# How many cache pages each unit of the prompt's attention takes: by its blocks, or by what its blocks leave of an even share

## The reference

```python
# prompt: 4 heads x 8 blocks of 128 queries, causal
s = einsum('bqhmd,bkhmd->bmhqk', q, k) * scale + bias(q_pos - k_pos)
p = softmax(s); attn = p[:, 0] - lam * p[:, 1]; out = attn @ v
# the 8 sequences ("decode"): the same, on 4096 cached tokens each
kp = cache_k[l][page_table]   # 32 pages of 128 tokens a sequence
vp = cache_v[l][page_table]
```

## Time and profile before

| what | us |
|---|---|
| median of three runs (lowest, highest) | 1438.85 (1438.1, 1441.78) |
| the profiled execution | 1434.25 |
| its span | 1432.4 |
| TensorE busy in the span | 1269.2 |
| VectorE busy | 626.4 |
| ScalarE busy | 369.1 |
| waits of VectorE for key pages, 620 to 880 us | 31.0 |

### The profile page before, as it was taken

How to read it: one execution, slowest core, us unless ns; L and a number is a source line. 1 busy time by engine, 2 the same in 40 slices (tenths; PEclk the granted TensorE clock), 3 DMA queues, 4 the chain that set the end, 5 groups by cost and what they waited for, 6 DMA issues and landing times.

```text
span 1432.4 us, 24206 instructions
## 1 busy us (share of the span) xinstructions
PE 1269.2 (89%) x9261; PEld 897.7 (63%) x9261; DVE 626.4 (44%) x1464; ACT 369.1 (26%) x758; POOL 123.5 (9%) x300
## 2 busy tenths in 40 slices
PE   6999998999898989986687877999897399999987
PEld 5666876667687778744454545455554288787852
DVE  4001415444464638366576775455424511212117
ACT  4021202111212225244355553222222011111113
POOL 4400000000000010110000000000000111111012
PEclk9999999999999999988798988999998599999998
DMA  7810011010020106776877979999980499999837
GB/s 244 291 52 30 30 38 36 30 61 1 17 74 18 45 7 216 233 256 200 289 246 266 314 270 351 385 317 338 320 272 31 148 313 304 300 307 302 281 118 303
DMA packets 158308, 274.03 MB, mean 191 GB/s; under 512 B 13448, under 2 KB 72752, under 8 KB 158208
## 3 DMA queue, kind: packets, MB, share of 16 engines
q1 hardware_dynamic: 139776, 217.46, 45.1%
q0 software_dynamic: 11648, 38.39, 7.7%
q10 hardware_dynamic: 6784, 16.85, 3.4%
HBM read 235.55 MB, written 37.09 MB: 190 GB/s over the span
## 4 chain that ended last, share of the span: by engine, by line
PE 70%; DVE 12%; SPq 5%; DMA 4%; ACT 4%; issue 4%; POOL 0%; DVEq 0%; ACTq 0%; POOLq 0%
PE bank L1060 16%; PE bank L1063 13%; PE bank L1484 10%; PE bank L1343 6%; PE bank L1504 4%; PE bank L1109 4%; DVE arena L1762 3%; DMA arena<-in_cache_k_dram 3%; PE bank L1186 3%; SPq L527 3%; PE bank L1229 2%; ACT arena L875 2%; PE bank L1037 1%; PE bank L1499 1%; PE bank L1469 1%
## 5 line engine op out<-in xcount | busy, mean ns | idle before, releaser
L1060 PE MATMUL bank<-arena 128*128 128x352 f32 x768 | 239.0, 470 | 0.0
L1762 DVE STREAM_TRANSPOSE arena<-arena 128x512 f32<-128x512 f32 x256 | 158.4, 677 | 95.3 <-DMA arena<-in_cache_k_dram 95.0
L1060 PEld LDWEIGHTS bank<-arena 128*128 128x128 f32 x768 | 147.4, 195 | 80.1 <-issue 5.9
L1063 PE MATMUL bank<-arena 128*128 128x256 f32 (+1 forms) x864 | 195.5, 384 | 0.6 <-issue 0.6
L1063 PEld LDWEIGHTS bank<-arena 128*128 128x128 f32 (+1 forms) x864 | 155.0, 182 | 33.2 <-issue 6.3
L1484 PEld LDWEIGHTS bank<-arena 128*128 128x128 f32 x1024 | 143.2, 193 | 9.2 <-issue 9.2
L1484 PE MATMUL bank<-arena 128*128 128x160 f32 x1024 | 144.2, 303 | 1.9 <-DVE arena L2074 1.9
L1343 PE MATMUL bank<-arena 128*128 128x512 f32 x256 | 121.0, 617 | 0.9 <-ACT arena L885 0.9
L1186 PE MATMUL bank<-arena,tab 128*32 128x256 f32 x1024 | 71.1, 424 | 17.0 <-DVE arena L1762 11.6
L741 ACT ACTIVATE arena<-bank 128x352 f32<-128x352 f32 x48 | 22.2, 463 | 232.1 <-PE bank L1060 232.1
L1343 PEld LDWEIGHTS bank<-arena 128*128 128x128 f32 x256 | 47.4, 195 | 54.8 <-issue 54.5
(11 more groups left out here) (342 smaller groups left out, 1494.3 us busy)
## 6 DMA issues: line engine op xcount, KB each, us to landing
arena<-in_cache_k_dram SPq DMA_DIRECT2D x256, 256.0 KB, 4.7
arena<-in_cache_v_dram SPq DMA_DIRECT2D x256, 256.0 KB, 4.0
arena<-in_expert_w_dram SPq DMA_DIRECT2D x48, 1024.0 KB, 7.5
arena<-in_w_in_dram SPq DMA_DIRECT2D x14, 1024.0 KB, 5.0
expert_scratch<-route POOLq DMA_DIRECT2D x40, 256.0 KB, 6.9
expert_scratch<-arena ACTq DMA_DIRECT2D x16, 512.0 KB
out_dram<-arena SPq DMA_DIRECT2D x12, 512.0 KB, 3.0
arena<-in_x_prompt_dram SPq DMA_DIRECT2D x4, 1024.0 KB, 9.2
```

Source lines behind the costliest of these rows:

```text
L1060: mm = nc.tensor.matmul(bank(g)[:, 0:N3], w[:, k, c * P:(c + 1) * P], hT[:, k * TOK + n * N3:k * TOK + (n + 1) * N3], start=(k == 0), stop ...
L1063: mm = nc.tensor.matmul(bank(g)[0:ROWS[c], 0:256], tok(hT, k, c), w[:, k, :], start=(k == 0), stop=(k == KC - 1))
L1762: V.transpose(page, page).then_inc(sem("k_flip"), 1)
```

## The change

`u_beat` is computed from another share. A unit's share of pages falls in a straight line with i, by 0.44 a block from (4.5 x 0.44 + 62/32), with a floor of 0.25; units of two parts halve it; the sum is scaled to the same 62 beats. All else, the order of the quads in the ring and the two other lists too, is as before.

```diff
-        blocks = [sum(units[n][1] + 1 if units[n][1] < 4 else 4 if part == 0 else units[n][1] - 3 for n, part in parts[:k + 1]) for k in range(len(parts))]
-        u_beat = [v_beat[-1] + round(62 * n / blocks[-1]) for n in blocks]
+        def share(i):
+            return (4.5 - i) * 0.44 + 62 / len(units)
+
+        pages_of = [max(share(units[n][1]), 0.25) / (2 if units[n][1] >= 4 else 1) for n, part in parts]
+        u_beat = [v_beat[-1] + round(62 * sum(pages_of[:k + 1]) / sum(pages_of)) for k in range(len(parts))]
```

## The result

The change makes the kernel slower: 1448.44 us (median of 7 executions, 1439.14 to 1453.99) against 1438.1 for the kernel before (7 executions of the same session). The ratio is 1.0078, with a 95% interval of 1.0044 to 1.0111, or some 11 us. The forecast was 1416 in a range of 1395 to 1440, so it was wrong in sign. One of all the executions in this document was slow and is left out of its kernel's figures (e18: 1562.42 us, at a mean clock of 0.815 where the others had 0.935 to 0.948).

What follows compares the result with a forecast made beforehand. No engine fills a head: late key pages and a three-engine chain take turns. Heads -23 us, residual waits +4, mixing entry -4 make -23: 1434.25 becomes 1411, plus 4.6 for the median 1416, range 1395 to 1440.

Steps and rivals of the forecast that it cites:

- residual waits: Attention heads: waits for keys that would remain after the change, 1 us a head, plus 4 us in the sum.
- the chain: Units 2 to 5: combine, biases, transposed quad, exps take turns on three engines; each first-part quad adds 2.49 us.
- Fewer beats in units 5 to 7.: Head 2: unit 5 minus 3 us; units 6 and 7, with four beats fewer, minus 4.3.
- Entry of the mixing.: Start of the mixing stage: a ring left full by unit 7 gives back 0 to 7.9 us, 4 taken.
- The wait of 4.99 goes, since the ring was refilled during large units with few beats.: Unit 2 of head 2: VectorE's 4.99 us wait for keys disappears; the unit's net is minus 0.5 us.
- no change: Rival, chance 0.10: transfers pause in units 5 to 7, waits return in units 1 to 3, 6 us a head; 1436.
- The batch's end comes here. That costs 0 to 3.7, I take 2.: Unit 2 of head 2: the batch's softmax flips and previous batch's keep move here from unit 5, plus 2 us.
- Head 1.: Minus 12 us: wait -9, unit 0 +1.3, unit 1 +3, chain -5, units 6 and 7 -4.3, batch's end +2.
- Head 0.: Minus 5 us: units 0 and 1 get six quads and take about 20, plus 11; later units give more back.
- Head 3 has the same counts: Head 3 was taken to have head 2's counts of beats and quads, so also minus 3 us.
- VectorE piles up: Rival, chance 0.12: quads ahead of combine in units 0 to 2 make TensorE wait; +24 us, 1463.
- The clock: Rival, chance 0.10: waits in units 0 and 1 lower TensorE's clock in heads 1 to 3, +5 us each; 1431.

Runs made afterwards that it cites:

- e18: e10 with every key quad transposed two beats ahead of its own beat (three for the first of a pair): 1418.85 us, ratio 0.9897.
- e5: The kernel before with a quarter of every page loaded (32 of 128 rows): 1405.59 us, ratio 0.9779.
- e7: The kernel before with a quarter of each key page transposed (128 of 512 columns): 1404.59 us, ratio 0.9764.
- e13: The kernel before with a quarter of each page loaded and a quarter of each key page transposed: 1379.08 us, ratio 0.9598.
- e9: The kernel before with VectorE's transposes of a unit's first part put behind the second part of the bias: 1437.35 us, ratio 1.0021.
- e10: The kernel before with an equal share of pages per unit and transposes put behind the second bias: 1412.85 us, ratio 0.987.
- e4: The kernel before with the change's shares in head 3 only: 1440.5 us, ratio 1.003.
- e15: e3 with a quarter of every page loaded: 1415.45 us, ratio 0.9835.
- e6: The change with a quarter of every page loaded: 1429.07 us, ratio 0.993.
- e3: The change with five u_beat limits moved so no key pair is transposed and multiplied in the same unit: 1435.73 us, ratio 0.9986.

## Why the prediction was wrong, step by step

**Head by head.** Without the 4 us of residual waits the forecast had -5, -12, -3 and -3 us for heads 0 to 3; they were +3.4, -1.5, +14.3 and +2.8. The terms below make most of this.

**What bounds the kernel.** Right as far as it went: the chain and the supply of pages take turns. With pages cut e5 gains 34 us, with transposes cut e7 gains 35, with both e13 57. The price of 2.49 us for a quad on the chain held in head 0, whose units 2 to 4 went from 32.6 to 26.4 us (forecast minus 5.5), and not in head 1; e9, which takes every such quad off the chain, gains nothing. The Trainium skill's "Optimize this engine first" (Perfetto Trace Analysis, "Identifying the Most-Contended Engine") gave no direction here: e10 takes no work from any engine, moves only the order and gains 1.3%. That such a change would bring nothing was my inference; the page does not say it.

**Fewer beats in units 5 to 7.** Right. The forecast took -3 for unit 5 and -4.3 for units 6 and 7 of head 2; they were -1.4 and -1.2 there, but units 6 and 7 of heads 1 and 3 gave 6.4 and 4.5, and units 4 to 7 of all heads 27.1 together.

**Entry of the mixing.** The mechanism was right, and so was the size: by the 64th matmul the change is 4.6 us ahead, for 4 forecast, and e4 has the same with head 3 alone. That the stretch is 9 us shorter is 4 us more than the entry; they come with low-clock stretches that the kernel before has later on, and that were no term of mine. I have no run that says why they went.

**"The wait of 4.99 goes, since the ring was refilled during large units with few beats."** Failed. I had checked that 11 quads fit into 35 us. The average holds; the times don't. At most six quads are ahead, up to three of them already asked for by the transposes; units 0 and 1 of head 2 take six beats in 12.5 us, and SP can put back a quad in 2 to 3.5 us of its own, only once a place is free. So the store was gone by unit 2, and the wait was 7.11 us instead of 4.99. In the four heads VectorE waited 26.5 us where I had left 4. The transfers' pause moved to units 4 and 5 (0.09 and 0.38 of the DMA engines), and the waits stood in unit 2 of the heads again (6.71 us in head 3). That is the rival "no change" in its mechanism and nearly in its price of 24 us; the units it named for the pause were 5 to 7.

**"The batch's end comes here. That costs 0 to 3.7, I take 2."** This step failed most. Unit 2 of head 2 was to take 13.5 - 5.0 + 2.5 + 2 = 13.0 us, and took 23.1. Single executions with small loads take it apart: 8.7 us in e5, with one quad and no batch's end; 13.0 in e15, with one quad, the batch's end and a page 4.58 us late, but no meeting; 20.0 in e6, with a page 4.07 us late, the meeting, one quad more and one beat more. So the batch's end cost 4.3 us with that late page, and the step to e6 another 7.0 in the unit and 5.9 in the head, of which up to 2.5 are the quad; in it TensorE waited 7.87 us for a transpose. With whole pages the page was 7.11 us late, the wait 9.54 and the unit 23.1. That 13.0 stands in my sum and in e15 is chance: the sum has two quads, e15 one. The bound of 3.7 was TensorE's wait in head 0 for one small step of VectorE, not for a transpose. What a meeting can cost is everything ahead of the transpose on VectorE, which works in order: in the change the wait for the page, the normalise, a combine, a bias and the other quad, then matmuls at half the clock. The beat at which a pair is used could have been set against the list of units before any run: two units do both.

**Head 1.** The wait at unit 0 went as forecast (12.4 us to 3.5), and unit 1 grew by 5.3 us where 3 were forecast. But "two fewer on the chain, minus 5" and "the end of a batch in unit 2, plus 2" did not come: units 2 to 5 took 31.9 us before and 40.4 in the change. VectorE waited 6.25 and 1.71 us for the two quads that it transposes in its turn of unit 1, and TensorE, which multiplies this pair in unit 2, waited 5.35 us for the second. By the lists that is no meeting; an overdue transpose of the unit before costs like one.

**Head 0.** Its units 0 and 1 were to take 20 us and took 29.7 (12.7 and 17.0). I had added VectorE's busy time alone; six quads there stand ahead of the softmax's small steps, which three engines hand each other by turns (the wait of 7.60 us shown with e3). With small loads unit 1 is just as long (17.1), so pages are not the cause; with the even share it is 14.9, and with the transposes behind those steps 7.8 (e10). My "Head 3 has the same counts" as head 2 was wrong as well: by the lists its units take 3, 3, 2, 2, 2, 1, 1, 1 beats, and it has no meeting.

**The rivals.** "VectorE piles up" is what happened, with one cause more than I gave it, the late pages, and at 11 us in place of 24. Its point of decision, 41 us for units 0 to 3 of heads 1 to 3, was drawn badly: 38.3, 44.5 and 38.0 were measured, one of the three over it, and the kernel is slower all the same, because that test left out head 0, whose units 0 to 3 grew by 15.6. "The clock" is a part of it: 10.1 us more of TensorE's busy time in the four heads, for the same matmuls. I had taken it as a case beside piling up; how much of it follows from the stalls is not shown. A chance of 0.12 for the pile-up was too small, given that the trace had a wait of 3.71 us of this kind in it and that I knew the change to bring more.

**What stays open.** How the 14.2 us of unit 2 in head 1 (6.9 before, 12.8 with small loads) divide into the batch's end and the overdue transpose was not tried. No run removes the meeting of head 2 and leaves its quads and beats where they are. Nor was there a version that keeps the change's shares and lets SP issue sooner, for instance by a larger ring.

## What to carry to other kernels

When background work is dealt out to a loop, an average that fits is not enough: add up, beat by beat, how many buffers are free against how fast the issuing engine can refill them, and count those that a look-ahead already holds. Then list the places where a step is produced and consumed within one turn or the next, for on engines that work in order each of them can cost all that stands between (waits of 9.54, 8.89 and 5.35 us here; 13 us came back by moving five limits by a beat or two). Here, where two limits took turns, an even share with the small steps ahead of the large ones beat a share that follows either limit.

## What the runs showed of the hardware

**The price of issuing.** In head 2 SP took 4.0 to 6.9 us for eight transfers of 256 KB (the change) and 3.9 to 6.3 us for eight of 64 KB (e5): some 0.5 to 0.9 us each. The shortest groups were 4.02 and 3.89 us for keys, 6.18 and 5.14 us for values. The small loads also have another pattern of rows, so bytes and pattern are not told apart. The Trainium skill (Perfetto Trace Analysis, "What 'DMA-bound' means") names the issuing sequencer as one of the things that a transfer-bound stretch can be bound on, with its track solidly filled. The trace agrees for the small units: from 765.1 to 789.0 us SP's four groups (6.31, 4.36, 6.88 and 4.02 us) fill 21.6 of 23.8 us, while over the whole attention SP waits 83 us for places.

**The granted clock moves with the order of the steps.** The same matmuls of the four heads kept TensorE busy 191.3 us in e10, 200.0 before and 210.2 in the change, at granted clocks by head of 0.88 to 0.92, 0.81 to 0.92 and 0.79 to 0.92. After TensorE's wait of 9.54 us the key matmuls took 3.64 us for 1.93. Then unit 3 ran at 1.00 and unit 4, almost free of page work, at 0.54; TensorE was idle 1.56 us in the one and 1.99 us at the start of the other. Whether the long stall had a part in that is open: without it unit 4 ran at 1.00 in e3 and at 0.68 in e15.
